# Expert 3's first weight chunks loaded early, and VectorE's selections moved ahead of the slot lists, in a two-layer trunk with a mixture of experts

## The chip, the cores and the metric

One core of a Trainium2 chip runs the whole program. The metric is the device time of one execution in microseconds (us); what is given is the median of several executions. The engines are TensorE (PE; its weight loads are PEld), VectorE (DVE), ScalarE (ACT), GpSimd (POOL) and SyncE (SP), which issues nearly all loads from device memory (HBM). Each engine runs its own instructions in order and waits on semaphores for the others.

## What is computed

512 tokens of width 1024 go through two layers and a last RMSNorm, all in float32. Layer 0 mixes tokens with a gated recurrence and chunked attention, layer 1 with a gated linear recurrence. Each layer then has a mixture of experts, which is where most of the time goes:

```python
h = h + mix
h = h + hier_moe(rms_norm(h, norm_ffn_g[layer]), router_group, router_expert, w_gate, w_up, w_down)

# hier_moe: 4 groups of 8 experts; top-1 group, then top-2 experts inside it, for every token
g_gate, g_idx = top_k(softmax(xt @ router_group), 1)
e_val, e_idx = top_k(logits of the 8 experts of that group, 2)
gate = g_gate * softmax(e_val)
for each of 32 experts e:                  # on the tokens that chose it
    hb = silu(xb @ w_gate[e]) * (xb @ w_up[e])   # w_gate, w_up: 1024 x 512
    y += gate * (hb @ w_down[e])                 # w_down: 512 x 1024
```

## The kernel before

**Experts.** The 32 experts are served one after another in both layers. Each has a list of at most 56 token slots (CAP). They go in groups of two (PICK): while group g is computed, the tokens of group g+1 are gathered. Gathering is a matmul of the tokens with a 0/1 matrix (times the norm's factor). VectorE writes that matrix (`selections(l, g)`, 8 instructions at L1657, into `me["sel"]`), TensorE multiplies (`pick`, L663, 64 matmul records a half, as 40 + 24 around the transpose), and VectorE copies the result out of PSUM with the norm's gain (`take_pick`, L1825). There is one `me["sel"]`, so selections of group g+2 can be written only when both halves of group g+1 have been picked.

For expert e, TensorE runs `gate_up` (L828: gate and up projections, 32 records), the first part of a `pick`, `turn` (L834: the transpose of the hidden rows), the rest of the `pick` and `out_rows` (L843: the down projection). Between them ScalarE takes silu (`silu`, L1306), VectorE multiplies (`hidden`, L1874) and copies the transpose (L1901), and at the end ScalarE (L1321) and VectorE (L1883) each copy half of the expert's rows to `me["rows"]`, from which GpSimd scatters them to device memory (`scatter_rows`, L1491). `me["rows"]` has two halves, used in turn, so the rows of expert 2 wait until the scatter of expert 0 has landed (`scattered[0]`).

**Lists.** GpSimd needs the table of row numbers. `slot_lists` (VectorE, L1839 to L1844) builds two operands from all tokens' places, `slot_table` (TensorE, L852 and L854, right after `gate_up` of expert 2) multiplies them, and `row_table` (VectorE, L1853 to L1861) turns the product into numbers (`table_ready`, on which GpSimd's first scatter waits) and also hands ScalarE the router's logits (`route_in`), for an Exp (L1367) behind its part of expert 2's rows.

VectorE's order is that of `dve_expert`: at expert 1 it does `take_pick`, `slot_lists`, `row_table`, its half of expert 1's rows (`out_rows`), and then `selections(l, 2)`, on which TensorE's first `pick` at expert 2 waits.

**Weights.** The three matrices of an expert, 2048 KB each, sit in slots of a ring of nine (`EXPERT_SLOTS`, three experts). SyncE issues the loads in one fixed order (`moe_loads`, L459 whole matrices, L493 pieces), each behind a wait for the matmuls that last read the slot: expert e's gate and up behind `gate_up` of expert e-3, its down behind `out_rows` of e-3. For experts 3 to 5 the loads are cut in pieces (`piece`), some released halfway through `gate_up` (`gu_half`).

**Start.** The program begins with the norm of x: TensorE transposes (`turn_rows`, L612), and ScalarE (`take_turned`, L1203, four instructions a half tile) and VectorE (`turned_rows`, L1603, one instruction a half tile) copy the transposes to `xT`, ScalarE tile 1, VectorE tiles 0, 2 and 3. The first projection (`proj0`, L736) needs all of `xT` and the first 2048 KB of its weights (L408).

## Time and profile before

| | |
|---|---|
| median of 3 executions | 1600.71 us (1599.98 to 1601.44) |
| the profiled execution | 1600.28 us, of which its span 1598.6 us |
| PE busy | 1541.1 us, 96% of the span |
| DVE, ACT, POOL busy | 554.0, 345.8 and 210.7 us |
| loads of SyncE's queue | 462.51 MB, 70.3% of what 16 DMA engines could be busy |
| mean granted TensorE clock | 0.994 of full speed |

The page cuts the span in 40 slices of 40 us. TensorE shows 9 tenths in nearly all of them, so the profile has to be read by what little TensorE waits for, and by the slices in which the DMA engines are as full: slices 10 to 18 and 31 to 39, within the experts, at 422 to 428 GB/s. Times in the rows below count from the span's start. A matmul of float32 shows as two records.

### The profile page before, as it was taken

The page shows a single profiled execution, that of the slowest core. Times are in us where ns is not written, and L with a number is a line of the kernel's source. Part 1 is how long each engine was busy: PE and PEld are TensorE (multiplying, and loading weights), DVE is VectorE, ACT ScalarE, POOL GpSimd, SP SyncE. Part 2 cuts the span into 40 slices and gives each one's busy share as a digit, 9 for nine tenths or more (in the row PEclk, how much of TensorE's full clock was granted, in tenths as well). Part 3 has the DMA queues.
Part 4 walks back from the last instruction along what each step waited for, and adds up shares of the span by engine and source line. Part 5 has one row for each costly group of instructions (what it writes and reads, how often), then busy time and mean ns, then how long its engine had stood idle before and what let it go on. Part 6 is the DMA issues. An engine that isn't in the chain of part 4 may idle for free. (4 is left out here: it accounts for less than half of the span.)

```text
span 1598.6 us, 26973 instructions
## 1 busy us (share of the span) xinstructions
PE 1541.1 (96%) x11592; PEld 794.0 (50%) x11592; DVE 554.0 (35%) x1277; ACT 345.8 (22%) x577; POOL 210.7 (13%) x256
## 2 busy tenths in 40 slices
PE   7999999999999999998999999999999999999997
PEld 4444545544444444443566666646454444444442
DVE  4222635322232222225254444445322222222225
ACT  3131621010000000003444555432010000000003
POOL 5000000000000000000244444420000000000000
PEclk9999999999999999999999999999999999999999
DMA  8711056999999999997421112115989999999996
GB/s 294 257 70 53 27 235 268 399 373 427 426 427 426 427 426 427 426 422 309 176 88 54 54 63 96 56 53 224 372 359 426 428 425 426 426 427 427 427 422 271
DMA packets 59403, 472.22 MB, mean 295 GB/s; under 512 B 12929, under 2 KB 12937, under 8 KB 31376
## 3 DMA queue, kind: packets, MB, share of 16 engines
q1 hardware_dynamic: 54336, 462.51, 70.3%
q0 software_dynamic: 4800, 7.87, 1.3%
q8 instruction: 95, 1.56, 0.4%
q14 instruction: 28, 0.23, 0.0%
q10 hardware_dynamic: 144, 0.05, 0.0%
HBM read 452.03 MB, written 24.27 MB: 298 GB/s over the span
## 5 line engine op out<-in xcount | busy, mean ns | idle before, releaser
L828 PE MATMUL ps<-sb_ring,sb_work 128*56 128x512 f32 x2048 | 451.6, 593 | 16.5 <-issue 13.3
L828 PEld LDWEIGHTS ps<-sb_ring,sb_work 128*56 128x56 f32 x2048 | 146.4, 130 | 308.3 <-issue 308.0
L663 PE MATMUL ps<-sb_work,sb_h 128*64 128x112 f32 x4096 | 225.1, 264 | 7.5 <-DVE sb_work L1657 7.5
L843 PE MATMUL ps<-sb_ring,sb_work 128*56 128x512 f32 x1024 | 230.8, 593 | 1.2 <-DMA sb_ring<-in_w_down_dram 1.2
L663 PEld LDWEIGHTS ps<-sb_work,sb_h 128*64 128x64 f32 x4096 | 207.2, 139 | 42.2 <-issue 30.9
L1491 POOL DMA_INDIRECT expert_rows<-sb_work,sb_ri x60 | 54.7, 912 | 1124.9 <-DVE sb_work L1883 1113.6
L1874 DVE TENSOR_TENSOR sb_work<-sb_work,ps 56x512 f32<-56x512 f32 x64 | 70.2, 1097 | 314.7 <-ACT sb_work L1306 314.6
L1069 PE MATMUL ps<-sb_work,sb_ring 128*128 128x512 f32 x384 | 172.3, 603 | 2.0 <-ACT sb_work L1203 2.0
L1306 ACT ACTIVATE sb_work<-ps 56x512 f32<-56x512 f32 x64 | 37.6, 588 | 441.8 <-PE ps L828 441.8
L843 PEld LDWEIGHTS ps<-sb_ring,sb_work 128*56 128x56 f32 x1024 | 67.1, 130 | 114.2 <-issue 112.0
L1321 ACT ACTIVATE sb_work<-ps 56x512 f32<-56x512 f32 x60 | 35.4, 590 | 395.1 <-PE ps L843 395.1
L1069 PEld LDWEIGHTS ps<-sb_work,sb_ring 128*128 128x128 f32 x384 | 71.7, 191 | 86.9 <-issue 86.0
L736 PE MATMUL ps<-sb_work,sb_ring 128*128 128x512 f32 x256 | 110.3, 592 | 1.7 <-DMA sb_ring<-in_ab_w_in_dram 1.7
L1883 DVE COPY sb_work<-ps 56x512 f32<-56x512 f32 x60 | 41.6, 693 | 188.3 <-ACT sb_work L1321 188.2
L736 PEld LDWEIGHTS ps<-sb_work,sb_ring 128*128 128x128 f32 x256 | 48.6, 190 | 62.6 <-issue 62.6
L2144 DVE COPY_PREDICATED sb_ring<-sb_tables,ps 128x512 f32<-128x512 uint32 x48 | 35.6, 742 | 93.5 <-PE ps L1087 92.7
L663 PE MATMUL ps<-sb_ring,sb_work 128*64 128x128 f32 x1120 | 64.3, 273 | 0.0
L663 PEld LDWEIGHTS ps<-sb_ring,sb_work 128*64 128x64 f32 x1120 | 60.9, 137 | 1.9 <-issue 1.9
L1657 DVE TENSOR_SCALAR sb_work<-sb_iota,sb_slot_key,sb_rstd 128x56 f32<-128x56 f32 x256 | 61.1, 308 | 0.3
L1825 DVE TENSOR_TENSOR sb_work<-ps,sb_fg 128x448 f32<-128x448 f32 x64 | 40.0, 625 | 59.6 <-PE ps L663 59.4
L1540 POOL TENSOR_TENSOR sb_ring<-sb_ring 128x256 f32<-128x256 f32 x56 | 48.6, 867 | 89.0 <-ACT sb_ring L1376 50.5
L628 PE MATMUL ps<-sb_ring,sb_work 128*128 128x512 f32 x128 | 59.5, 599 | 0.0
(240 smaller groups left out, 1216.2 us busy)
## 6 DMA issues: line engine op xcount, KB each, us to landing
sb_ring<-in_w_down_dram SPq DMA_DIRECT2D x62, 2048.0 KB, 24.4
sb_ring<-in_w_gate_dram SPq DMA_DIRECT2D x54, 2048.0 KB, 21.8
sb_ring<-in_w_up_dram SPq DMA_DIRECT2D x54, 2048.0 KB, 26.4
sb_ring<-in_w_gate_dram SPq DMA_DIRECT2D x18, 1024.0 KB, 10.5
sb_ring<-in_w_up_dram SPq DMA_DIRECT2D x18, 1024.0 KB, 12.8
sb_ring<-in_c_w_in_dram SPq DMA_DIRECT2D x8, 2048.0 KB, 9.0
sb_ring<-in_ab_w_in_dram SPq DMA_DIRECT2D x5, 2048.0 KB, 12.0
expert_rows<-sb_work SPq DMA_DIRECT2D x2, 4096.0 KB, 19.9
```

The source lines that it names most:

```text
L628: mm = nc.tensor.matmul(bank(job)[:], y[:, c, t * P:(t + 1) * P], wblock(s, NC)[:, c, :], start=(c == 0), stop=(c == NC - 1))
L663: mm = nc.tensor.matmul(dst[64 * z:64 * z + 64], a[:, 64 * z:64 * z + 64], b, start=start, stop=stop)
L736: mm = nc.tensor.matmul(dst[:], a, b, start=(c == 0), stop=(c == NC - 1))
L828: mm = nc.tensor.matmul(dst[64 * z:64 * z + CAP, :], me["xgT"][:, j, c, q * CAP:(q + 1) * CAP], wblock(slots[z], NC)[:, c, :], start=(c == ...
L843: mm = nc.tensor.matmul(dst[64 * z:64 * z + CAP, :], src[:, c * CAP:(c + 1) * CAP], wblock(slots[2], FC)[:, c, z * 512:(z + 1) * 512], sta ...
L1069: mm = nc.tensor.matmul(dst[:], w[:, c, k, :], xT[:, c, :], start=(c == 0), stop=(c == NC - 1))
L1491: return g.indirect_dma_start(out=y_d[l], out_offset=bass.IndirectOffsetOnAxis(ap=idx, axis=0), in_=me["rows"][0:CAP, j, :], in_offset=Non ...
L1540: g.tensor_tensor(qk[:, :, 0:m], kk[:, :, 0:m], e[:, :, 0:m], ALU.mult)
L1657: return v.tensor_scalar(dst, iota[:, 0:CAP], slot_key[:, t, e:e + 1], rstd[:, 2 * l + 1, t:t + 1], ALU.is_equal, ALU.mult)
L1825: drains(v.tensor_tensor(me["xgT"][:, g % 2, CB * b:CB * b + CB, :], bank(job)[:, 0:CB * PICK * CAP].rearrange("p (c s) -> p c s", c=CB), ...
L1874: return v.tensor_tensor(me["hrow"][0:CAP, :].rearrange("p (c q) -> p c q", c=FC), chunked(me["silu"][64:64 + CAP, :], FC), chunked(ps[moe ...
L1883: drains(v.tensor_copy(half_row(me["rows"][0:CAP, e % 2, :], 1), chunked(bank(("dn", l, e))[64:64 + CAP, :])), ("dn", l, e))
```

## The change

Three things are changed.

1. Chunk 0 (of eight) of expert 3's gate and up matrices, 128 x 512 elements (256 KB) each, is loaded to two free places in `work` (`ahead`), right behind the last load of expert 2 and with no wait for a slot; `gate_up` of expert 3 reads its first chunk there, behind a wait on `ahead_in`. The first piece of expert 3 in the ring is then chunk 1 alone.
2. VectorE's order at experts 1 and 2: `selections(l, 2)` stands right behind the `take_pick` of expert 1, ahead of `slot_lists`; `row_table` moves from expert 1 to expert 2, behind `hidden(l, 2)`.
3. At the start, the second half of tile 3 of `xT` is copied by ScalarE instead of VectorE.

```diff
--- before.py
+++ after.py
@@ -198,6 +198,7 @@
         me.update(carve(high, [("sel", (NT, PICK * ROW))]))
         me.update(carve(low[:, 2 * NC * PICK * CAP:], [("A", (2, NT, CAP))]))
         me.update(carve(high[:, 2 * D:], [("spread", (NT, NE))]))
+        ahead = (low[:, 7 * T:8 * T], high[:, T:2 * T])
         fin_g = tables[:, 0:D]
         fin_c = ring[:, 0, D:2 * D]
         hg = ring[:, 3, :].rearrange("p (t d) -> p t d", t=NT)
@@ -244,7 +245,7 @@
         out_ready, out_stored = [sem(f"out_ready{t}") for t in range(NT)], sem("out_stored")
         h_made = sem("h_made")
         zero_made, zero_out, attn_zero = sem("zero_made"), sem("zero_out"), sem("attn_zero")
-        gu_half = sem("gu_half")
+        gu_half, ahead_in = sem("gu_half"), sem("ahead_in")
         half_in = {(e, part): sem(f"half_in{e}_{part}") for e, part in HALVES}
         late_ready, fin_ready, hg_ready = sem("late_ready"), sem("fin_ready"), [sem(f"hg_ready{t}") for t in range(NT)]
 
@@ -493,8 +494,10 @@
                         sp.dma_start(ring[:, s, lo * 512:hi * 512], by_partition(w[l, e:e + 1])[:, lo * 512:hi * 512]
                                      ).then_inc(ring_in[s], 16)
 
+                for dst, w in zip(ahead, (w_gate, w_up)):
+                    sp.dma_start(dst, by_partition(w[l, 3:4])[:, 0:512]).then_inc(ahead_in, 16)
                 sp.wait_ge(gu_half, 4 * l + 1)
-                piece(3, 0, 2)
+                piece(3, 1, 2)
                 sp.wait_ge(gu_half, 4 * l + 2)
                 piece(3, 2, 4)
                 wait_full(sp, ("gu", l, 0))
@@ -820,13 +823,14 @@
             out_proj(0, w0_in[5:7], m0["y"], ([NC, NC, NC, NC - 1], [0, 0, 0, 0]))
 
 
-            def gate_up(l, slots, j, q, cs=range(NC), k=7):
+            def gate_up(l, slots, j, q, cs=range(NC), k=7, first=None):
 
                 dst = ps[moe_bank(l, k)]
                 for c in cs:
                     for z in range(2):
-                        mm = nc.tensor.matmul(dst[64 * z:64 * z + CAP, :], me["xgT"][:, j, c, q * CAP:(q + 1) * CAP],
-                                              wblock(slots[z], NC)[:, c, :], start=(c == 0), stop=(c == NC - 1))
+                        w = first[z] if first and c == 0 else wblock(slots[z], NC)[:, c, :]
+                        mm = nc.tensor.matmul(dst[64 * z:64 * z + CAP, :], me["xgT"][:, j, c, q * CAP:(q + 1) * CAP], w,
+                                              start=(c == 0), stop=(c == NC - 1))
                 return mm
 
             def turn_hidden(l):
@@ -895,7 +899,9 @@
                     if q == 0:
                         for b in range(PB):
                             wait_drained(pe, ("pick", l, g, b))
-                    mm = gate_up(l, three, g % 2, q, range(0, 4))
+                    if e == 3:
+                        pe.wait_ge(ahead_in, 32 * (l + 1))
+                    mm = gate_up(l, three, g % 2, q, range(0, 4), first=ahead if e == 3 else None)
                     if e == 2:
                         mm.then_inc(gu_half, 1)
                     fills(gate_up(l, three, g % 2, q, range(4, 8)), ("gu", l, e))
@@ -1183,6 +1189,7 @@
                     square(0, t, xs[:, t, :], xh[:, t, :])
                 act.wait_ge(vec_in, 16)
                 take_turned(0, 1)
+                take_turned(0, NT - 1, (1,))
 
             def norm_mid():
 
@@ -1193,9 +1200,9 @@
                 take_turned(2, 0)
                 take_turned(2, 1)
 
-            def take_turned(n, t):
-
-                for half in range(2):
+            def take_turned(n, t, parts=(0, 1)):
+
+                for half in parts:
                     job = ("xt", n, t, half)
                     wait_full(act, job)
                     for c in range(4):
@@ -1593,10 +1600,10 @@
                     src, dst = h[:, t, :].rearrange("p (c q) -> p c q", c=NC), chunked(xh2[:, t, :])
                 v.tensor_scalar(dst, src, rstd[:, n, t:t + 1], None, ALU.mult).then_inc(xh_ready, 1)
 
-            def turned_rows(n, t):
+            def turned_rows(n, t, parts=(0, 1)):
 
                 gain = at["mix_g"]
-                for half in range(2):
+                for half in parts:
                     job = ("xt", n, t, half)
                     c0 = (n // 2) * NC + half * 4
                     wait_full(dve, job)
@@ -1699,8 +1706,8 @@
                 if t == 1:
                     dve.wait_ge(vec_in, 16)
                     turned_rows(0, 0)
-            for t in range(2, NT):
-                turned_rows(0, t)
+            turned_rows(0, 2)
+            turned_rows(0, NT - 1, (0,))
             v.memset(m0["xa"][:, :, 0:3], 0.0).then_inc(dve_made, 1)
             dve.wait_ge(rtab_in, 16)
             v.tensor_copy(m0["rtab"][0:HEADS_B, 0:255], m0["rtab"][0:HEADS_B, 255:256].broadcast_to([HEADS_B, 255])
@@ -1895,6 +1902,8 @@
                 g, q = e // PICK, e % PICK
                 if e != 1:
                     hidden(l, e)
+                if e == 2:
+                    row_table(l)
                 wait_full(dve, ("ht", l, e))
                 if e > 0:
                     wait_full(dve, ("dn", l, e - 1))
@@ -1903,14 +1912,14 @@
                     hidden(l, 1)
                 take_pick(l, g + 1, q)
                 if e == 1:
+                    selections(l, g + 2)
                     slot_lists(l)
-                    row_table(l)
                 if e == 3:
                     gate_values(l)
                 if e == 4:
                     late_gates(l)
                 out_rows(l, e)
-                if q == PICK - 1 and g + 2 < NE // PICK:
+                if e > 1 and q == PICK - 1 and g + 2 < NE // PICK:
                     selections(l, g + 2)
 
             def last_hidden(l, e):
```

VectorE at expert 1, before, from the `take_pick` on to the first instruction of `row_table`:

```order
L1825 TENSOR_TENSOR sb_work<-ps,sb_fg 128x448
L1839 TENSOR_TENSOR sb_work<-sb_slot_key,sb_work 128x128
L1840 TENSOR_REDUCE sb_place<-sb_work 128x4
L1841 TENSOR_TENSOR sb_work<-sb_work,sb_tokval 128x128
L1839 TENSOR_TENSOR sb_work<-sb_slot_key,sb_work 128x128
L1840 TENSOR_REDUCE sb_place<-sb_work 128x4
L1841 TENSOR_TENSOR sb_work<-sb_work,sb_tokval 128x128
L1844 TENSOR_TENSOR sb_work<-sb_iota,sb_place 128x224 x2
L1853 TENSOR_REDUCE sb_top<-ps 128x1
```

and after the change:

```order
L1832 TENSOR_TENSOR sb_work<-ps,sb_fg 128x448
L1664 TENSOR_SCALAR sb_work<-sb_iota,sb_slot_key,sb_rstd 128x56 x8
L1846 TENSOR_TENSOR sb_work<-sb_slot_key,sb_work 128x128
L1847 TENSOR_REDUCE sb_place<-sb_work 128x4
L1848 TENSOR_TENSOR sb_work<-sb_work,sb_tokval 128x128
L1846 TENSOR_TENSOR sb_work<-sb_slot_key,sb_work 128x128
L1847 TENSOR_REDUCE sb_place<-sb_work 128x4
L1848 TENSOR_TENSOR sb_work<-sb_work,sb_tokval 128x128
L1851 TENSOR_TENSOR sb_work<-sb_iota,sb_place 128x224 x2
L1890 COPY sb_work<-ps 56x8x64
```

The eight instructions of `selections(l, 2)` now come first, and the rows' copy (L1883, now L1890) directly behind `slot_lists`.

VectorE from the end of `row_table` into expert 2, before:

```order
L1861 TENSOR_TENSOR sb_ex<-sb_ex,sb_rstd 128x20
L1883 COPY sb_work<-ps 56x8x64
L1657 TENSOR_SCALAR sb_work<-sb_iota,sb_slot_key,sb_rstd 128x56 x8
L1874 TENSOR_TENSOR sb_work<-sb_work,ps 56x512
L1901 COPY sb_work<-ps 128x224
```

and after the change, from the copy of expert 1's rows on:

```order
L1890 COPY sb_work<-ps 56x8x64
L1881 TENSOR_TENSOR sb_work<-sb_work,ps 56x512
L1860 TENSOR_REDUCE sb_top<-ps 128x1
L1861 TENSOR_SCALAR sb_flag<-sb_top 128x1
L1862 COPY sb_work<-ps 56x32
L1864 TENSOR_SCALAR sb_work<-sb_work 56x32
L1865 SCALAR_TENSOR_TENSOR sb_work<-sb_work 56x32
L1867 CAST sb_ri<-sb_work 56x32
L1868 TENSOR_TENSOR sb_ex<-sb_ex,sb_rstd 128x20
L1910 COPY sb_work<-ps 128x224
```

The seven instructions of `row_table` now stand between `hidden` of expert 2 (L1881) and the copy of its transposed rows (L1910), on which TensorE's down projection waits.

SyncE's loads from expert 2's up matrix to the second piece of expert 3, layer 0, with what they wait for, before:

```order
L459 DMA sb_ring<-in_w_up_dram 128x4096 [waits filled5]
L493 DMA sb_ring<-in_w_gate_dram 128x1024 [waits gu_half]
L493 DMA sb_ring<-in_w_up_dram 128x1024
L493 DMA sb_ring<-in_w_gate_dram 128x1024 [waits gu_half]
L493 DMA sb_ring<-in_w_up_dram 128x1024
L493 DMA sb_ring<-in_w_gate_dram 128x2048 [waits filled5]
L493 DMA sb_ring<-in_w_up_dram 128x2048
```

and after the change:

```order
L460 DMA sb_ring<-in_w_up_dram 128x4096 [waits filled5]
L498 DMA sb_work<-in_w_gate_dram 128x512
L498 DMA sb_work<-in_w_up_dram 128x512
L494 DMA sb_ring<-in_w_gate_dram 128x512 [waits gu_half]
L494 DMA sb_ring<-in_w_up_dram 128x512
L494 DMA sb_ring<-in_w_gate_dram 128x1024 [waits gu_half]
L494 DMA sb_ring<-in_w_up_dram 128x1024
L494 DMA sb_ring<-in_w_gate_dram 128x2048 [waits filled5]
L494 DMA sb_ring<-in_w_up_dram 128x2048
```

Two loads of 128 x 512 to `work` go out with no wait, and the two behind the first `gu_half` are half as long.

## Rows read from the trace of the kernel before

**Rows 1.** The list of TensorE's waits, whole span: us, times, longest us.

```profile
PE ps L828 <- issue: 13.3, 12, 3.1
```

**Rows 2.** TensorE in time, layer 0, experts 2 and 3: start, us, records, idle before.

```profile
300.61 7.04 PE L828 MATMUL ps<-sb_ring,sb_work 128*56 128x512 f32 x32
...
307.92 1.01 PE L854 MATMUL ps<-sb_work 128*56 128x32 f32 x16
312.72 3.61 PE L663 MATMUL ps<-sb_work,sb_h 128*64 128x112 f32 x40 [3.79 <-DVE sb_work L1657]
...
321.27 7.04 PE L828 MATMUL ps<-sb_ring,sb_work 128*56 128x512 f32 x32
328.13 2.09 PE L663 MATMUL ps<-sb_work,sb_h 128*64 128x112 f32 x40
330.20 0.42 PE L834 MATMUL ps<-sb_ident,sb_work 56*128 56x56 f32 x4
```

**Rows 3.** VectorE in time, layer 0, experts 1 and 2.

```profile
297.94 0.28 DVE L1839 TENSOR_TENSOR sb_work<-sb_slot_key,sb_work 128x128 f32<-128x128 f32 x1
...
299.88 0.69 DVE L1844 TENSOR_TENSOR sb_work<-sb_iota,sb_place 128x224 f32<-128x224 f32 x2
308.97 0.19 DVE L1853 TENSOR_REDUCE sb_top<-ps 128x1 f32<-128x32 f32 x1 [8.40 <-PE ps L854]
...
310.19 0.69 DVE L1883 COPY sb_work<-ps 56x512 f32<-56x512 f32 x1
310.80 1.86 DVE L1657 TENSOR_SCALAR sb_work<-sb_iota,sb_slot_key,sb_rstd 128x56 f32<-128x56 f32 x8
```

**Rows 4.** TensorE in time, layer 1, the same place.

```profile
1158.58 3.77 PE L663 MATMUL ps<-sb_work,sb_h 128*64 128x112 f32 x40 [3.75 <-DVE sb_work L1657]
```

**Rows 5.** Stretches, layer 0: PE, PEld, DVE, ACT, POOL busy; clock, DMA share, GB/s.

```profile
314.00:316.00 2.00, 2.00 (x28) 2.00 (x26) 0.00 (x0) 0.00 (x0) 0.00 (x0) 0.56 1.02 403
...
318.00:322.00 4.00, 4.00 (x21) 1.24 (x18) 0.62 (x1) 0.52 (x1) 0.00 (x0) 1.00 0.16 60
...
328.00:330.00 2.00, 2.00 (x42) 1.86 (x38) 1.03 (x1) 0.59 (x1) 0.00 (x0) 1.00 0.82 197
330.00:332.00 2.00, 2.00 (x36) 1.67 (x33) 0.47 (x3) 0.00 (x0) 0.00 (x0) 1.00 0.79 319
332.00:344.00 12.00, 12.00 (x88) 5.02 (x84) 4.98 (x16) 1.18 (x2) 0.91 (x1) 1.00 1.00 428
```

**Rows 6.** SyncE's issues in time: expert 5's down, expert 6's gate, expert 7's gate.

```profile
321.48 0.33 SPq L459 DMA_DIRECT2D sb_ring<-in_w_down_dram  x1
328.35 0.33 SPq L459 DMA_DIRECT2D sb_ring<-in_w_gate_dram  x1
...
342.27 0.33 SPq L459 DMA_DIRECT2D sb_ring<-in_w_gate_dram  x1
```

**Rows 7.** TensorE in time, layer 0: its first wait for weights.

```profile
600.76 7.08 PE L828 MATMUL ps<-sb_ring,sb_work 128*56 128x512 f32 x32 [0.58 <-issue]
```

**Rows 8.** ScalarE in time, layer 0: expert 2's rows, and the last table load behind them.

```profile
321.49 0.59 ACT L1321 ACTIVATE sb_work<-ps 56x512 f32<-56x512 f32 x1 [13.20 <-PE ps L843]
...
323.62 1.28 ACT L1306 ACT_TABLE_LOAD   x1
```

**Rows 9.** Line L1491: layer 0's first scatter and its landing; last row, all sixty.

```profile
L1491 POOL DMA_INDIRECT expert_rows<-sb_work,sb_ri x1: 1105/1105/1105, 311.1 to 311.1; - x1
...
DMA to landing us min/median/max: 7.2/7.2/7.2
...
DMA to landing us min/median/max: 5.6/8.0/9.3
```

**Rows 10.** TensorE in time: the last pick ahead of expert 0, both layers.

```profile
268.80 0.41 PE L693 MATMUL ps<-sb_work,sb_tri 128*128 128x32 f32 x2 [2.02 <-DVE sb_work L1645]
...
269.36 3.29 PE L663 MATMUL ps<-sb_work,sb_h 128*64 128x112 f32 x64
...
1113.20 0.41 PE L693 MATMUL ps<-sb_work,sb_tri 128*128 128x32 f32 x2 [2.02 <-DVE sb_work L1645]
...
1113.76 4.95 PE L663 MATMUL ps<-sb_work,sb_h 128*64 128x112 f32 x64
```

**Rows 11.** The start, in time: VectorE's last copies, and the first projection.

```profile
12.40 1.89 DVE L1603 TENSOR_TENSOR sb_work<-ps,sb_vec 128x512 f32<-128x512 f32 x3
...
14.89 0.67 PE L736 MATMUL ps<-sb_work,sb_ring 128*128 128x512 f32 x1 [1.66 <-DMA sb_ring<-in_ab_w_in_dram]
```

## The prediction

> **What bounds the kernel now.** TensorE is busy for 96% of the span, so I read only what it waits for, and then ask for each wait whether its end would pass through to the end of the layer. First the list of TensorE's waits. Its largest entry is 13.3 us in 12 waits at `gate_up`, put down to "issue" [rows 1]; in time the first of them in layer 0 comes at 600.8 us, late in the layer [rows 7], and they stand where an expert's weights have not landed: one expert takes TensorE 13.9 us (the gates of experts 6 and 7, released by `gate_up` of 3 and 4, go out at 328.35 and 342.27) [rows 6], while its three matrices (6.29 MB) take 14.7 us at the 428 GB/s that the full queue moves [rows 5]. TensorE begins each layer ahead of the loads, loses 0.8 us of that lead per expert, and is held by them for its last experts.
>
> So the time in TensorE alone says nothing; a wait early in a layer is worth only what it also moves the queue of loads. The stretches tell that: at 318 to 322 us the queue is nearly empty (60 GB/s), it has a second hole at 328 to 332 (197 and 319 GB/s), and from 332 on it is full [rows 5]. In the holes it is SyncE that waits, for slots: expert 5's down goes out at 321.48, when `out_rows` of expert 2 is done, and expert 6's gate at 328.35, when `gate_up` of expert 3 is done [rows 6]. Whatever delays TensorE before 328 us delays the whole queue behind expert 6, and so the end of the layer.
>
> Exactly there lies the wait that the change is about. In layer 0 TensorE ends `slot_table` at 308.93 and stands 3.79 us until VectorE has written the selections of group 2 [rows 2]; layer 1 has the same wait with 3.75 us [rows 4]. VectorE had been free, but it had `slot_lists`, `row_table` (which waits 8.40 us for TensorE's `slot_table`) and a copy of rows in front of them [rows 3].
>
> **The change: VectorE's order.** In the new order `selections(l, 2)` begins where `slot_lists` began, at 297.94, and takes 1.86 us [rows 3]: ready at 299.8, when TensorE needs it at 308.9. The wait goes, 3.79 us in layer 0 and 3.75 in layer 1. With it goes a second cost: after the wait the first 40 records of the pick took 3.61 and 3.77 us where those of expert 3 take 2.09 [rows 2, 4], and the granted clock at 314 to 316 us is 0.56 [rows 5]: after the idle stretch it stood for most of this pick at half, 1.2 GHz. Without the idle I take the pick of expert 3 as the price. That gives 1.52 and 1.68 us more. A last 0.18 us is the overlap of a pick with the matmuls before it (it starts at 328.13, they end at 321.27 + 7.04 = 328.31), which the wait had prevented. Sum: 3.79 + 1.52 + 0.18 = 5.5 us in layer 0, 3.75 + 1.68 + 0.18 = 5.6 us in layer 1.
>
> What is late next? `slot_lists` (297.94 to 300.57, 2.63 us) moves behind the selections, to 302.4; `slot_table` needs it when `gate_up` of expert 2 ends, 300.61 + 7.04 = 307.65 [rows 2, 3]. 5 us to spare, cost nothing. `row_table` (308.97 to 310.19, 1.2 us) moves behind `hidden` of expert 2. In expert 3 the transpose starts 1.9 us after the end of `gate_up` (328.31 to 330.20) and finds `hidden` done [rows 2], so in expert 2 `hidden` is done by 309.5 and `row_table` by 310.7, while the transpose itself, behind 2.09 us of pick, cannot end before 311.2. VectorE's copy of it, for which TensorE's down projection waits, is not delayed. Cost nothing, with 0.5 us of cover; a TensorE wait of some tenths if the cover is gone.
>
> **Does the queue follow?** Expert 6's gate goes out 5.5 us earlier, at 322.85. Before, the queue by then had run dry; now expert 5's down, issued at 316.0, still stands behind the pieces of expert 5, which end near 318.6 (318 to 322 moves 60 x 4 us = 0.24 MB, 0.56 us of full rate). Down takes 2.10 MB / 428 = 4.9 us, to 323.5. From issue to full flow a load on an empty queue needs about 1.3 us: of expert 6's 1.03 MB moved by 332 (197 x 2 + 319 x 2) full rate would take 2.4 us, 329.6, against the issue at 328.35 [rows 5, 6]. So expert 6 flows from 322.85 + 1.3 = 324.15, behind the 323.5 at which the queue is clear: TensorE still sets it, and the queue moves by the full 5.5 us. Thereafter it is full as before (expert 7's gate would go out at 336.8, expert 6's matrices last to 324.15 + 14.7 = 338.9). The waits at the end of the layer keep their length and come 5.5 us earlier. Layer 1 has the same rows and the same sum, 5.6 us.
>
> **The two chunks ahead.** They move 0.52 MB (1.2 us at 428 GB/s) out of the stretch that ends at 318.6. That would be worth 1.2 us if the queue set the start of expert 6; by the lines above it does not, by 0.65 us without the chunks and by up to 1.9 us with them. They are cover and no gain: 0, between 0 and 0.6 us a layer should the flow start later than I read it. Nor does TensorE need expert 3 earlier. The two loads that are left of the first piece are shorter, and two more loads are issued, each about the 0.33 us of SyncE's other issues [rows 6], before a wait that SyncE has anyway.
>
> All of this hangs on a queue that can run dry: it moves 428 GB/s when full, and has its holes at 318 and 328 us [rows 5]. A rule of the Trainium skill says otherwise. The page "DMA: Bandwidth & Descriptors" (section "Where 436 GB/s comes from") holds that for loads from device memory the memory's share of one core, about 358 GB/s, is what binds. By that estimate an expert's weights would take 17.6 us, the queue would never be empty, and the sum would be 0 instead of 11.1 us (rival (d)); by this the trace disagrees.
>
> **The start.** ScalarE's four copies of the last half tile replace one of VectorE's three, which end at 12.40 + 1.89 = 14.29 us. The projection starts at 14.89, on its weights [rows 11]. Four ScalarE copies after the last transpose cannot end much later than 14.4. Nothing, between -0.2 and +0.2 us.
>
> **Sum.** 5.5 + 5.6 = 11.1 us. The profiled execution took 1600.28 us (span 1598.6), so 1589.2; it lies 0.4 us under the median of 1600.71, and from that the forecast is **1589.6 us**.
>
> **Rivals.**
>
> (a) *ScalarE is late at expert 3.* Its half of expert 2's rows waits for the scatter of expert 0 (`scattered[0]`), and that for `row_table`, which now ends 0.5 us later in time while all of TensorE is 5.5 us earlier. The first scatter was issued at 311.1 and landed 7.2 us later, 318.3 [rows 9]: in the new order 318.8, after `out_rows` of expert 2 (316.0). Behind it ScalarE has the rows, Exp and two table loads, 3.4 us (321.49 to 323.62 + 1.28) [rows 8], to 322.2; silu of expert 3 is due at 322.8. Free by 0.6 us, plus what slack the transpose has. But landings range from 5.6 to 9.3 us, median 8.0 [rows 9]: at 9.3 ScalarE is free at 324.3, and TensorE would wait 1.3 to 1.5 us in each layer. Time: 1592.4.
>
> (b) *Slower than before*, by the same chain and beyond a point: if the scatter's landing, now in a fuller queue, took so long that TensorE stood as long as before with the clock halved again. A loss of 5.5 us less 1.6 for the clock is 3.9 us of wait, a landing of 311.6 + 12 us or later. At 14.5 us it waits 6.4, loses 1.6 to the clock and gives 2.5 us a layer away: 1605.7. Sixty landings, none over 9.3, speak against it.
>
> (c) *The queue follows only in part.* If 256 KB loads run less well than 512 KB ones, or the lag after an issue is longer, expert 6 starts up to 1 to 2 us later than reckoned: gain 7 to 9 instead of 11.1, 1592 to 1593.7.
>
> (d) *The change doesn't do what it says at the end of the layer*: the queue is never short of work, the loads set the end wholly, and the wait comes back there. 1600.7, no change. The holes of [rows 5] speak against it.
>
> (e) *The clock at the other wait.* Ahead of `positions` of the last tile TensorE idles 2.02 us in both layers; behind it the pick of 64 records takes 3.29 us in layer 0 and 4.95 in layer 1, at half the clock there [rows 10]. Everything in layer 1 comes earlier now, and this may fall out either way: 1.7 us less, 1587.9, or in layer 0 1.7 us more, 1591.3. The skill's page "TensorE: Matmul & The Clock Gate" (section "What's actually happening") says that the gate watches activity on a rhythm of its own, not started by the kernel, so that the same idle can fall on either side; that bears on this chance and on nothing else.
>
> **How the numbers follow.** Forecast, with its tenths: 0.65. (a) 0.08. (b) 0.03. (c) 0.10. (d) 0.03. (e) 0.09. Something that I don't see, either side: 0.02. From the bounds, (e) below and (c) above, the range is 1587.5 to 1593.7; it leaves out (b), (d) and the unseen. A measurement of this kernel can tell about 0.2% (3.2 us) from no change; all but (b), (d) and half of the unseen are faster by more: 0.93, no change 0.03, slower 0.04.
>
> **What the profile after would show.** No wait of TensorE at the pick of expert 2 in either layer, and 40 records in 2.1 us; the list of waits without the 7.5 us at L663; expert 6's gate issued near 322.9 instead of 328.35; no hole at 318 to 322, a smaller one before expert 6; the waits at the layer's end as long as before. Wrong if TensorE waits for ScalarE or VectorE at the transpose of expert 3, if the late waits grow by what the early one lost, or if expert 6's first bytes come later than 1.5 us after the issue.

## The result

| | before | after |
|---|---|---|
| median of the executions, us | 1600.35 (1598.77 to 1601.44, 4) | 1590.97 (1590.47 to 1591.31, 4) |
| the profiled execution, us | 1600.28 | 1590.47 |
| its span, us | 1598.6 | 1588.7 |

The ratio is 0.9942, with a 95% interval of 0.9925 to 0.9959: faster by 9.4 us, where 11.1 were forecast (1589.6, range 1587.5 to 1593.7). The direction, the place and the mechanism were right; the sum was 1.2 us too large by the spans, 1.7 us by the medians.

TensorE in time, layer 0, experts 2 and 3, after the change (start, us, line, records):

```profile
308.15 0.96 PE L858 MATMUL ps<-sb_work 128*56 128x32 f32 x15
...
309.00 2.11 PE L666 MATMUL ps<-sb_work,sb_h 128*64 128x112 f32 x39
311.04 0.46 PE L838 MATMUL ps<-sb_ident,sb_work 56*128 56x56 f32 x4
...
316.06 1.03 PE L832 MATMUL ps<-sb_work 128*56 128x512 f32 x4
316.91 6.18 PE L832 MATMUL ps<-sb_ring,sb_work 128*56 128x512 f32 x28
322.92 2.09 PE L666 MATMUL ps<-sb_work,sb_h 128*64 128x112 f32 x40
```

These answer to [rows 2]: the pick behind `slot_table` no longer waits, and 39 of its records take 2.11 us instead of 3.61 for 40. The four records that read `sb_work` alone are expert 3's first chunk from `ahead`. Layer 1 reads the same (before: [rows 4]):

```profile
1149.43 2.11 PE L666 MATMUL ps<-sb_work,sb_h 128*64 128x112 f32 x39
```

VectorE, layer 0 (before: [rows 3]). The selections, the end of `slot_lists`, `hidden`, the first and last of `row_table`, and the copy of the transpose:

```profile
298.17 1.83 DVE L1664 TENSOR_SCALAR sb_work<-sb_iota,sb_slot_key,sb_rstd 128x56 f32<-128x56 f32 x8
...
301.85 0.69 DVE L1851 TENSOR_TENSOR sb_work<-sb_iota,sb_place 128x224 f32<-128x224 f32 x2
...
308.55 1.07 DVE L1881 TENSOR_TENSOR sb_work<-sb_work,ps 56x512 f32<-56x512 f32 x1 [4.59 <-ACT sb_work L1313]
309.65 0.19 DVE L1860 TENSOR_REDUCE sb_top<-ps 128x1 f32<-128x32 f32 x1
...
310.68 0.17 DVE L1868 TENSOR_TENSOR sb_ex<-sb_ex,sb_rstd 128x20 f32<-128x20 f32 x1
311.53 0.39 DVE L1910 COPY sb_work<-ps 128x224 f32<-128x224 f32 x1 [0.69 <-PE ps L838]
```

`row_table` is done 0.69 us before the transpose is there: the cover that I put at 0.5 us.

The stretches of layer 0 (before: [rows 5]). Columns: PE, PEld, DVE, ACT, POOL busy; clock, DMA share, GB/s:

```profile
318.00:320.00 2.00, 2.00 (x12) 0.63 (x10) 0.14 (x1) 0.75 (x2) 0.00 (x0) 1.00 1.12 436
320.00:322.00 2.00, 2.00 (x12) 0.60 (x10) 0.55 (x1) 1.97 (x3) 0.15 (x1) 1.00 1.02 434
322.00:324.00 2.00, 2.00 (x30) 1.36 (x28) 0.24 (x1) 1.25 (x2) 0.76 (x1) 1.00 0.93 389
324.00:325.00 1.00, 1.00 (x22) 0.82 (x19) 0.86 (x1) 0.00 (x0) 0.00 (x0) 1.00 0.94 299
325.00:326.00 1.00, 1.00 (x20) 0.94 (x20) 0.39 (x1) 0.00 (x0) 0.00 (x0) 1.00 0.90 328
326.00:327.00 1.00, 1.00 (x20) 0.71 (x18) 0.22 (x1) 0.00 (x0) 0.00 (x0) 1.00 1.01 393
327.00:328.00 1.00, 1.00 (x8) 0.40 (x6) 0.90 (x5) 0.00 (x0) 0.00 (x0) 1.00 0.95 377
328.00:330.00 2.00, 2.00 (x13) 0.55 (x9) 0.26 (x2) 0.00 (x0) 0.00 (x0) 1.00 1.00 410
330.00:332.00 2.00, 2.00 (x12) 0.68 (x10) 1.11 (x4) 0.59 (x1) 0.00 (x0) 1.00 1.01 426
```

and SyncE's issues of expert 5's down and expert 6's gate (before: [rows 6]):

```profile
316.27 0.33 SPq L460 DMA_DIRECT2D sb_ring<-in_w_down_dram  x1
323.13 0.33 SPq L460 DMA_DIRECT2D sb_ring<-in_w_gate_dram  x1
```

The empty stretch at 318 to 322 us (60 GB/s) is full. Behind expert 6's issue a shallow hole is left: 299, 328, 393 and 377 GB/s in four us. What it costs is taken up with the run that loads expert 6 in halves. (The GB/s of these rows count all queues, GpSimd's scatters too.)

The waits of TensorE over the whole span, by line (busy us, mean ns, idle before). First two lines of before, then the same two of after:

```profile
L828 PE MATMUL ps<-sb_ring,sb_work 128*56 128x512 f32 x2048 | 451.6, 593 | 16.5 <-issue 13.3 <-DMA sb_ring<-in_w_up_dram 3.1
L843 PE MATMUL ps<-sb_ring,sb_work 128*56 128x512 f32 x1024 | 230.8, 593 | 1.2 <-DMA sb_ring<-in_w_down_dram 1.2
```

```profile
L832 PE MATMUL ps<-sb_ring,sb_work 128*56 128x512 f32 x2040 | 449.8, 593 | 17.7 <-issue 15.0 <-DMA sb_ring<-in_w_up_dram 2.6
L847 PE MATMUL ps<-sb_ring,sb_work 128*56 128x512 f32 x1024 | 230.8, 593 | 1.0 <-DMA sb_ring<-in_w_down_dram 1.0
L666 PE MATMUL ps<-sb_work,sb_h 128*64 128x112 f32 x4096 | 221.9, 262 | 0.0
```

The waits for weights grew, from 16.5 + 1.2 to 17.7 + 1.0 us: 1.0 us of what the picks gained came back at the end of the layers. The 7.5 us of waiting at the pick (L663, now L666) are 0.

For the rest I use one table. In each layer it counts from the start of `gate_up` of expert 0 and gives the start of `gate_up` of expert 3 and of expert 4, and the end of the experts (the first matmul at L993, in the changed kernel L999). Everything in it is from one profiled execution of each kernel. "Queue" is the time at which SyncE's loads have moved one fixed number of bytes (83 MB in layer 0, 309 MB in layer 1, some 97 us into the experts), counted from the packets of the trace (another way of counting them shifts all of a column by 0.1 to 0.2 us). Differences of some tenths between single executions say little.

| kernel | layer 0: exp. 3, exp. 4, queue, end | layer 1: exp. 3, exp. 4, queue, end |
|---|---|---|
| before | 48.50, 62.42, 99.68, 459.36 | 48.64, 62.57, 96.90, 459.22 |
| after | 43.06, 57.00, 94.53, 453.86 | 43.06, 57.01, 92.31, 454.61 |
| after, once more | 43.06, 57.00, 94.67, 454.33 | 43.06, 57.33, 91.84, 454.40 |
| new order, no chunks | 43.05, 57.00, 94.69, 454.14 | 43.06, 57.00, 92.89, 455.19 |
| chunks, old order | 48.62, 62.55, 99.81, 458.98 | 48.59, 62.52, 97.03, 461.12 * |
| start undone | 43.06, 56.99, 94.69, 454.66 | 43.05, 57.00, 92.12, 456.56 * |
| table kept at expert 1 | 44.33, 58.25, 95.77, 455.54 | 44.32, 58.24, 93.16, 459.49 * |
| table late | 43.05, 63.07, 98.98, 458.29 | 43.06, 62.51, 95.78, 458.17 |
| before + 8 matmuls | 50.24, 64.16, 101.36, 460.46 | 50.24, 64.18, 98.85, 462.20 * |
| before + 4 matmuls | 47.03, 60.98, 98.26, 457.50 | 47.00, 60.94, 95.34, 457.44 |
| after, expert 6 in halves | 43.01, 56.95, 94.02, 454.92 ** | 43.06, 57.11, 91.33, 453.94 |
| after + fillers of 4 | 43.06, 57.00, 94.34, 453.78 | 43.06, 56.99, 92.42, 458.25 * |
| after + fillers of 2 | 43.06, 57.00, 94.74, 454.18 | 43.06, 57.02, 92.50, 457.93 * |
| halves + fillers of 2 | 43.06, 57.00, 93.81, 453.04 | 43.06, 57.01, 91.30, 454.81 * |

\* with the clock at half behind a late wait for weights: it costs 1.5 to 1.7 us, but 2.8 to 3.0 us in three of them (start undone, table kept, fillers of 4), where the clock stayed at half longer; ** behind two.

The span of 1598.6 less 1588.7 is 9.9 us: 5.50 in layer 0's experts, 4.61 in layer 1's, less 0.23 by which this execution reached expert 0 later.

### The profile page after: what moved, and what is told of

Its sections match the earlier page's. It is cut to its first block and busy times, and to the rows that moved or that the text cites. A ratio compares the mean times of both kernels' runs of the same rounds, so it can differ in the third digit from the quotient of the medians.

```text
span 1588.7 us, 26982 instructions
## 1 busy us (share of the span) xinstructions
PE 1537.8 (97%) x11592; PEld 791.5 (50%) x11592; DVE 554.0 (35%) x1276; ACT 347.1 (22%) x581; POOL 210.2 (13%) x256
## 5 line engine op out<-in xcount | busy, mean ns | idle before, releaser
L832 PE MATMUL ps<-sb_ring,sb_work 128*56 128x512 f32 x2040 | 449.8, 593 | 17.7 <-issue 15.0
L666 PE MATMUL ps<-sb_work,sb_h 128*64 128x112 f32 x4096 | 221.9, 262 | 0.0
L666 PEld LDWEIGHTS ps<-sb_work,sb_h 128*64 128x64 f32 x4096 | 204.2, 138 | 34.4 <-issue 30.8
L1881 DVE TENSOR_TENSOR sb_work<-sb_work,ps 56x512 f32<-56x512 f32 x64 | 70.2, 1097 | 319.3 <-ACT sb_work L1313 319.2
L1890 DVE COPY sb_work<-ps 56x512 f32<-56x512 f32 x60 | 41.6, 693 | 194.4 <-ACT sb_work L1328 194.4
L666 PE MATMUL ps<-sb_ring,sb_work 128*64 128x128 f32 x1120 | 64.3, 273 | 0.0
L666 PEld LDWEIGHTS ps<-sb_ring,sb_work 128*64 128x64 f32 x1120 | 60.9, 137 | 1.9 <-issue 1.9
```

Of the source, the lines that this page charges most:

```text
L666: mm = nc.tensor.matmul(dst[64 * z:64 * z + 64], a[:, 64 * z:64 * z + 64], b, start=start, stop=stop)
L832: mm = nc.tensor.matmul(dst[64 * z:64 * z + CAP, :], me["xgT"][:, j, c, q * CAP:(q + 1) * CAP], w, start=(c == 0), stop=(c == NC - 1))
L1881: return v.tensor_tensor(me["hrow"][0:CAP, :].rearrange("p (c q) -> p c q", c=FC), chunked(me["silu"][64:64 + CAP, :], FC), chunked(ps[moe ...
L1890: drains(v.tensor_copy(half_row(me["rows"][0:CAP, e % 2, :], 1), chunked(bank(("dn", l, e))[64:64 + CAP, :])), ("dn", l, e))
```

## The experiments

**The changed kernel again**, no edit.

> The changed kernel once more, beside the kernel before and the three kernels that undo parts of it. In the two profiles its span is 9.9 us shorter (1598.6 to 1588.7), where 11.1 was forecast. Theory: the same 9 to 10 us here, 0.994 of the time before. If the missing 1.2 us were chance, it would come out nearer to 11.

Measured 1589.36 us (1588.02 to 1595.41, 6 executions; before, beside it, 1601.33), ratio 0.9933 (0.9919 to 0.9948). The mechanism repeats. TensorE in time, layer 1 at expert 3:

```profile
1164.05 0.43 PE L838 MATMUL ps<-sb_ident,sb_work 56*128 56x56 f32 x4 [0.33 <-DVE sb_work L1881]
```

Here rival (a) shows for once, 0.33 us. ScalarE's rows of expert 2, in the changed kernel:

```profile
319.24 0.59 ACT L1328 ACTIVATE sb_work<-ps 56x512 f32<-56x512 f32 x1 [10.72 <-DMA expert_rows<-sb_work,sb_ri]
...
321.38 1.28 ACT L1313 ACT_TABLE_LOAD   x1
323.14 0.59 ACT L1313 ACTIVATE sb_work<-ps 56x512 f32<-56x512 f32 x1 [0.48 <-PE ps L832]
```

ScalarE does wait for the scatter, and is free 0.48 us before silu of expert 3 is due (0.6 forecast). In layer 1 of this second execution the slack was used up.

**The order alone**, without the two chunks.

```diff
-                for dst, w in zip(ahead, (w_gate, w_up)):
-                    sp.dma_start(dst, by_partition(w[l, 3:4])[:, 0:512]).then_inc(ahead_in, 16)
                 sp.wait_ge(gu_half, 4 * l + 1)
-                piece(3, 1, 2)
+                piece(3, 0, 2)
```

> The changed kernel without the two chunks ahead: expert 3's first piece is two chunks in the ring again; VectorE's order and the start as changed. My prediction held the chunks to be cover and worth nothing (0 to 0.6 us a layer): same time as e1. Rival, from the trace after the change: the queue is still moving expert 5's down at 323.9 us when expert 6's gate was issued at 323.1, so the queue now sets expert 6's start, and without the chunks it starts up to 1.2 us later in each layer: 1 to 2.4 us slower than e1, and TensorE's waits at the layer's end longer by that.

Measured 1590.8 us (1588.74 to 1593.75), 0.9938 (0.9926 to 0.9950). The order brings the gain. Without the chunks the queue is where it was in layer 0 (94.69 against 94.53 and 94.67) and 0.6 to 1.0 us later in layer 1 (92.89 against 92.31 and 91.84); the layer's end is 0.6 to 0.8 us later there. Against three further kernels below that have the chunks and the same order (92.12 to 92.50) it is 0.4 to 0.8 us, and it is one execution without the chunks. By the time of the whole program the two can't be told apart.

**The chunks alone**, with the old order and the old start.

```diff
                 take_pick(l, g + 1, q)
                 if e == 1:
-                    selections(l, g + 2)
                     slot_lists(l)
+                    row_table(l)
```

> The kernel before plus the two chunks ahead alone: VectorE's order and the start as before. Theory: no gain (0, within 0.3 us), since the wait of 3.8 us at expert 2 stays and expert 6's gate is still issued late, at 328.3 us, on an empty queue. Rival (the chunks are what shortens the layer, the order is not): a gain of 2.4 us or more.

Measured 1599.37 us (1595.10 to 1602.43, 12 executions), 0.9991 (0.9980 to 1.0002): no difference that shows. TensorE, layer 0:

```profile
312.52 3.72 PE L666 MATMUL ps<-sb_work,sb_h 128*64 128x112 f32 x40 [3.79 <-DVE sb_work L1663]
```

The wait and the halved pick are those of [rows 2]. The chunks are no part of the gain in layer 0.

**The start undone**, VectorE again taking the half tile.

```diff
                 take_turned(0, 1)
-                take_turned(0, NT - 1, (1,))
```

> The changed kernel with the last half tile of xT copied by VectorE again, as before. Prediction: nothing, within 0.2 us. From the trace after: the first projection waits for ScalarE there and all of TensorE stands 0.2 us later up to expert 2 (269.03 against 268.80), so this should be 0.2 us faster than e1, at the edge of what can be seen; in its trace the first projection starts at 14.9 on its weights or at 14.4.

Measured 1590.7 us (1588.48 to 1593.66), 0.9939 (0.9926 to 0.9952). The first projection, first in the changed kernel, then with VectorE's copy back:

```profile
15.13 2.38 PE L739 MATMUL ps<-sb_work,sb_ring 128*128 128x512 f32 x5 [1.56 <-ACT sb_work L1210]
```

```profile
14.74 2.81 PE L739 MATMUL ps<-sb_work,sb_ring 128*128 128x512 f32 x6 [1.60 <-DVE sb_work L1609]
```

ScalarE's copies can be what the projection waits for, which I had excluded. But over all profiled executions the projection starts between 14.24 and 15.20 us with ScalarE's copies (mean of nine 14.88) and between 14.70 and 15.06 with VectorE's (mean of five 14.83). This edit is worth nothing that can be told.

**The table kept at expert 1**: the selections go ahead, `row_table` stays where it was.

```diff
                     selections(l, g + 2)
                     slot_lists(l)
+                    row_table(l)
```

> The changed kernel with row_table back at expert 1, behind slot_lists; selections stay ahead of both. It tells the two moves of VectorE apart. Theory: the selections alone take the 3.8 us wait away, but VectorE then stands at row_table until slot_table is done (309.2 us), does it (1.2 us), copies expert 1's rows (0.7) and only then does hidden of expert 2 (1.1): done near 312.2, where TensorE wants to transpose at 311.0. A wait of about 1.1 us at the transpose of expert 2 in each layer, and a time about 2 us over that of the changed kernel. If the place of row_table didn't matter: the same time, no wait.

Measured 1592.59 us (1589.71 to 1596.52), 0.9948 (0.9931 to 0.9966). TensorE at the transpose of expert 2, layer 0:

```profile
313.90 0.42 PE L838 MATMUL ps<-sb_ident,sb_work 56*128 56x56 f32 x4 [1.23 <-DVE sb_work L1881]
```

`row_table` waits for TensorE's `slot_table`, and the rows' copy and `hidden` stand behind it. Expert 3 starts at 44.33 instead of 43.06 in the table, and the end of layer 0 follows (455.54, which is 1.2 and 1.7 us later than in the two executions of the changed kernel). So the move of `row_table` is worth 1.27 us a layer at expert 3. It is the smaller part of the gain; moving the selections alone brings 4.2 of 5.4 us. The time of the whole program doesn't show the 2 us that were expected: its interval overlaps with those of the changed kernel.

**The table late**: `row_table` behind `take_pick` of expert 2, which delays GpSimd's first scatter by 3.6 us (315.39 us against 311.8).

```diff
-                if e == 2:
-                    row_table(l)
                 wait_full(dve, ("ht", l, e))
...
                 take_pick(l, g + 1, q)
+                if e == 2:
+                    row_table(l)
```

> The changed kernel with row_table later still, behind the take_pick of expert 2: it ends near 315.6 instead of 310.7 us. This puts a price on my rival (a)/(b), the chain from row_table over GpSimd's first scatter and ScalarE's rows of expert 2 to silu of expert 3. Theory: in the changed kernel ScalarE is free 0.5 us before silu of expert 3 is due, so 4.9 us more make silu 4.4 us late; TensorE waits about 4.2 us at the transpose of expert 3 in each layer, its clock is halved behind it (1.5 us more), and most of both comes through to the end: 8 to 11 us over the changed kernel, near the time of the kernel before. If the scatter doesn't hold ScalarE: no wait, the same time.

Measured 1597.93 us (1596.02 to 1602.14), 0.9990 (0.9977 to 1.0003): nearly all of the gain is gone. ScalarE, then TensorE at expert 3, layer 0:

```profile
324.10 0.59 ACT L1328 ACTIVATE sb_work<-ps 56x512 f32<-56x512 f32 x1 [15.73 <-DMA expert_rows<-sb_work,sb_ri]
```

```profile
329.35 0.63 PE L838 MATMUL ps<-sb_ident,sb_work 56*128 56x56 f32 x4 [4.48 <-DVE sb_work L1881]
329.91 2.51 PE L666 MATMUL ps<-sb_work,sb_h 128*64 128x112 f32 x24
```

The landing is 4.86 us later than in the changed kernel; less the 0.48 us of slack that gives 4.4 us, and the wait is 4.48 (3.83 in layer 1). The clock halves behind it (24 records in 2.51 us instead of 1.37). This is the chain of rivals (a) and (b), shown with its price: each us of landing beyond the slack is a us of TensorE. In layer 0 expert 4 starts 6.07 us later, but the queue only 4.4 and the layer's end 4.0 to 4.4 us: expert 6's gate and up had been issued on time, and only its down, behind `out_rows` of expert 3, came late. The hole in the queue is now there:

```profile
334.00:336.00 2.00, 2.00 (x12) 0.60 (x10) 0.00 (x0) 0.00 (x0) 0.00 (x0) 1.00 0.50 205
336.00:338.00 2.00, 2.00 (x12) 0.60 (x10) 1.18 (x4) 0.59 (x1) 0.00 (x0) 1.00 0.73 156
```

**The wait filled in the kernel before**, first with eight matmuls, later with four. Their product is not used; they are work added. The first run's fill, the second had 4 in place of 8:

```diff
                     if e == 2:
                         slot_table(l)
+                        fill(moe_bank(l, 2), 8)
...
+            def fill(bank_, n):
+                for _ in range(n):
+                    nc.tensor.matmul(ps[bank_][:], ident[:], h[:, 0, 0:512], start=True, stop=True)
```

> The kernel before with 8 matmuls of 512 columns (their result isn't used) between slot_table and the pick of expert 2, about 3.5 us, within the wait for the selections. It parts the two terms of my sum: the wait stays where it ends (312.7 us), but TensorE is busy in it. Theory: the granted clock is not halved behind it, the first 40 records of the pick take 2.1 us instead of 3.6 and 3.8, expert 3 starts 1.5 us earlier in each layer and the kernel is 2.5 to 3.2 us faster than before. If the slow pick had another cause: no change.

> The kernel before, with four matmuls of 128 x 512 (their product is not used; they add work and change no output) on TensorE between slot_table and the pick of expert 2, in the 3.8 us in which it waits for VectorE. In the run with eight of them a matmul took 0.89 us, so four take 3.6 us and end just before the selections are ready. Theory: the half clock behind the wait is the price of idling alone, and is worth 1.52 + 1.68 us. So no wait above 0.3 us at that pick, its first 40 records in 2.1 us in both layers, expert 3 starting 47.1 us after expert 0 (48.5 in the kernel before, 43.06 after the change), and about 3 us faster than before, 1597.5. Rival: the clock at that place does not hang on this idle stretch, or what it costs comes back at the end of the layer: 1600.5, as before.

Eight: 1603.14 us (1601.34 to 1606.79), 1.0022 (1.0012 to 1.0031). Four: 1597.45 us (1594.62 to 1600.37, 11 executions; before, beside it, 1599.47), 0.9984 (0.9973 to 0.9995). TensorE, layer 0, with eight and with four:

```profile
308.74 7.13 PE L851 MATMUL ps<-sb_h,sb_ident 128*128 128x512 f32 x16
315.80 2.14 PE L663 MATMUL ps<-sb_work,sb_h 128*64 128x112 f32 x40
```

```profile
309.02 3.70 PE L851 MATMUL ps<-sb_h,sb_ident 128*128 128x512 f32 x8
312.88 2.14 PE L663 MATMUL ps<-sb_work,sb_h 128*64 128x112 f32 x40 [0.16 <-DVE sb_work L1663]
```

Eight missed their aim: I had sized them by `gate_up`, whose matmuls take 0.44 us each, and these take 0.89. They outlast the wait by 3.3 us, and expert 3 starts only 1.6 to 1.7 us later, since the pick behind them has its full clock. Four fit the wait. The wait is as long as before, the pick takes 2.14 us, expert 3 starts 1.47 and 1.64 us earlier (forecast of the prediction for the clock: 1.52 and 1.68), and the layers end 1.9 and 1.8 us earlier. So the second term of the sum is confirmed by itself, on the kernel before, and it passes through to the end. The time of the program agrees as far as its interval goes: 2.0 us of 3 expected.

**Fillers at the waits of 2.0 us in the changed kernel**: ahead of `positions` of the last tile in both layers, and ahead of layer 1's first projection. First with four matmuls each, later with two.

```diff
                 pick_first(l, 1)
+                fill(moe_bank(l, 2), 4)
                 positions(l, NT - 1)
...
-            xT_ready(2)
+            xT_ready(2, (0,))
+            fill(bk.jobs["xt", 2, 0, 0][0], 4)
+            xT_ready(2, range(1, NT))
```

> The changed kernel with 4 matmuls of 512 columns (result not used, about 1.8 us) ahead of two waits of 2.0 us that are still there: at positions of the last tile in each layer, and between the layers ahead of the first projection of layer 1. Theory: behind each of these waits the clock is halved in some executions (at 746 and 1108 us in the profile after; at 746 alone in e1) and costs 1.7 us each time; filled, it is never halved: 1.7 to 3.4 us faster than the changed kernel, and with less spread between executions. If they only delay TensorE: the same or slower.

> The changed kernel with the same three fillers of two matmuls alone. With four matmuls they took 3.7 us and outlasted the waits by 0.7 to 1.6 us each. Theory: with two (1.8 us) nothing is outlasted, the pick of 64 records behind positions takes 3.3 us in both layers, and the time is that of the changed kernel's undisturbed executions, 1590, with less spread between them. Rival: 1591 and the same spread, because the half clock then falls on another wait (the 3.1 us for weights at the end of layer 1).

Four: 1591.11 us (1590.03 to 1593.43), 0.9943 (0.9926 to 0.9959), too long again by the same factor. Two: 1588.53 us (1585.24 to 1589.67), 0.9917 (0.9903 to 0.9932). The last tile of layer 1, TensorE in time, in the changed kernel and with fillers of two:

```profile
1107.92 0.41 PE L696 MATMUL ps<-sb_work,sb_tri 128*128 128x32 f32 x2 [2.01 <-DVE sb_work L1652]
...
1108.69 4.68 PE L666 MATMUL ps<-sb_work,sb_h 128*64 128x112 f32 x64
```

```profile
1103.71 1.98 PE L705 MATMUL ps<-sb_h,sb_ident 128*128 128x512 f32 x4
...
1106.36 3.29 PE L667 MATMUL ps<-sb_work,sb_h 128*64 128x112 f32 x64
```

From the end of layer 0's experts to `gate_up` of expert 0 in layer 1 it is 386.57 us in the changed kernel and 383.06 with the fillers, 3.5 us less. The two halvings are 3.0 of it: with the chunks alone, where neither wait halved the clock, this stretch takes 383.55 us. Of these only a part reaches the end. Layer 1's end comes 3.3 us later behind expert 0 (457.93 against 454.61), 1.7 of it because the clock now halves behind the 3.3-us wait for the weights of expert 30, the last but one, most of the rest by longer waits for weights before it, one of 2.43 us at expert 23 above all, which I can't explain: the queue as a whole is no later there. Comparing medians against the kernel before of the same chip, 10.9 us are gained where the changed kernel gained 9.4 and 12.0; by those intervals the fillers alone are not told apart from nothing.

**Expert 6 in halves**: its gate and up are loaded as two pieces each, the first released halfway through `gate_up` of expert 3.

```diff
-                for e in range(6, NS):
+                sp.wait_ge(gu_half, 5 * l + 5)
+                piece(6, 0, 4)
+                wait_full(sp, ("gu", l, 3))
+                piece(6, 4, 8)
+                wait_full(sp, ("dn", l, 3))
+                weight_load(l, 6, 2)
+                for e in range(7, NS):
...
-                    if e == 2:
+                    if e in (2, 3):
                         mm.then_inc(gu_half, 1)
```

> The changed kernel, with expert 6's gate and up loaded in halves, the first half released halfway through gate_up of expert 3 instead of at its end. In the changed kernel the load queue moves 299, 328, 393 and 377 GB/s in the four us behind 324 us and 389 in the two ahead, which against 425 is 0.95 us of full flow lost in layer 0 up to 332 us, and 1.0 us in layer 1. Theory: this hole is why the end of the layer came 0.4 to 0.9 us less early than expert 3 did. So no stretch of a us under 380 GB/s between 318 and 332 us, the end of the layer 0.6 to 1.0 us nearer to expert 0 than in the changed kernel (453.86 and 454.61 us behind its gate_up there) as long as the clock is full in it, and 1 to 2 us faster, about 1589. Rival: the queue is held elsewhere (expert 4's down at 302 us, the landing of single loads), the layer keeps its 453.9 us and more, and the time is that of the changed kernel, 1591.

Measured 1588.78 us (1587.78 to 1591.92), 0.9922 (0.9908 to 0.9935). The stretches of its layer 0 (all of it 1.1 us later in this execution):

```profile
322.00:324.00 2.00, 2.00 (x12) 0.59 (x10) 0.09 (x1) 1.97 (x3) 0.61 (x1) 1.00 0.92 393
324.00:325.00 1.00, 1.00 (x22) 0.95 (x20) 0.12 (x1) 0.79 (x2) 0.30 (x1) 1.00 1.10 467
325.00:326.00 1.00, 1.00 (x24) 0.92 (x20) 0.98 (x1) 0.00 (x0) 0.00 (x0) 1.00 0.81 328
326.00:327.00 1.00, 1.00 (x18) 0.84 (x16) 0.39 (x1) 0.00 (x0) 0.00 (x0) 1.00 1.02 393
327.00:328.00 1.00, 1.00 (x20) 0.82 (x18) 0.10 (x1) 0.00 (x0) 0.00 (x0) 1.00 0.99 397
```

The hole is halved, not closed: one us at 328 GB/s is left. The queue is 0.5 us earlier in layer 0 and 1.0 in layer 1 (0.65 and 0.5 against the second execution of the changed kernel), and layer 1's end, with a full clock in all three, comes at 453.94 instead of 454.61 and 454.40. So the hole behind expert 6's issue did hold the queue by 0.5 to 1.0 us, and the end of layer 1 by 0.5 to 0.7; layer 0's end can't be read in this execution, with two halvings of the clock in it. The time of the whole program is not told apart from the changed kernel's: the intervals overlap.

**Halves and fillers of two together.**

> The changed kernel with expert 6's halves as in the run beside it, and with two matmuls of 128 x 512 (product not used) on TensorE in each of the three stretches in which it waits 2.0 us: ahead of positions of the last tile in both layers, and ahead of layer 1's first projection. Two take 1.8 us. Theory: those 2.0 us halve TensorE's clock for the 1.6 us behind in some executions and not in others; with them filled it is never halved there, the slower executions go, and the median falls by about 1 us below the run beside it, 1588. Rival: the fillers end after the wait by some tenths each, and the clock is halved elsewhere instead, so the time is the same or 0.5 us worse.

Measured 1586.52 us (1584.25 to 1587.05), 0.9907 (0.9894 to 0.9921). On the same chip its slowest execution lies below the fastest of the halves alone (1587.78), so the fillers do bring something when the queue follows, some 2 us. It is faster than both kernels. Against the changed one the comparison is across chips, by the ratios to the kernel before: 0.9907 here, 0.9942 and 0.9933 there, which is 4 to 6 us; the interval of the first of these two doesn't meet this one's, that of the second just does (0.9919 to 0.9921).

## Why the prediction came out right, and where its sum was off

**The wait and the clock behind it**: right, with their sizes. Expert 3 starts 5.44 and 5.58 us earlier, against 5.5 and 5.6. The order alone brings it, the chunks don't, and filling the wait shows the clock's share by itself, 1.47 and 1.64 us.

**The lists and `row_table`**: right. `slot_lists` ended at 302.5 (302.4 said), 5.3 us early; the cover of `row_table` was 0.69 us (0.5 said).

**"So the queue moves by the full 5.5 us"**: this is the step that failed, by size. Expert 6's gate was issued at 323.13, as reckoned (322.85, plus the 0.23 us of this execution). But I had the queue clear of expert 5 0.65 us behind that issue (323.5), so that a lag of 1.3 us would end on an empty queue and everything would be set by TensorE. In fact there was more of expert 5 left: at the issue 0.45 MB (layer 0) and 0.57 MB (layer 1), counted from the packets, 1.1 and 1.3 us at 428 GB/s, as long as the lag itself. The old loads' tail and the new loads' beginning meet at 299 to 393 GB/s. Before, 0.04 MB were left at that point, and the issue found a dry queue. The traces agree with that: where under 0.1 MB was left (eight layers of the kernels with the old order), the first 1 MB of expert 6 had been moved 4.2 to 4.3 us behind the issue; where 0.26 to 0.72 MB was left, 4.5 to 5.2 us, but for one layer (0.36 MB and 4.3 us); the two kernels with expert 6 in halves are left out here. The reckoning also left out a scatter of GpSimd's rows: its 0.12 MB move at 323 to 326 us, in the middle of this change-over, while before the change they fell into the hole at 328 us. How the loss divides between the backlog and the scatter no run shows. So the loads follow by 5.15 and 4.6 us (by 5.0 and 5.1 in the second execution of the changed kernel) instead of 5.5 and 5.6, and the layers' ends by 5.50 and 4.61 (5.03 and 4.82). The rest returns as waits for weights, 1.0 us in the list. In the profiled execution layer 0 kept its whole gain, 1.0 of the missing 1.2 us is layer 1's, and 0.23 the later arrival at expert 0. That was rival (c) in kind, at about half its price, and it goes with the queue's own backlog where I had named the loads' size and the lag. The loads in halves, which win back 0.5 and 1.0 us of the queue, show that the place is this one.

**The chunks**: 0 was said, 0 to 0.6 as the range. Layer 0: 0 to 0.2 us, but not for the reason given. The prediction took their 0.52 MB out of the stretch that ends at 318.6. By the packets the queue is 0.5 MB ahead with them 2 us before expert 0 (47.26 against 46.74 MB) and no longer ahead 10 us behind its start (48.94 against 49.10 MB): the slots for the next pieces come free at the same times with and without them (issues at 7.1 and 10.5 us), so the lead is used up in waiting for them. That this term came out right in layer 0 was luck. Layer 1: 0.4 to 1.0 us of the queue by one execution without them, at or over the end of the range; with the old order they bring nothing there either (97.03 against 96.90).

**The start**: nothing, and so it was in the mean (0.05 us). The reason was half wrong: in the profiled execution the projection waited for ScalarE and not for its weights.

**Rival (a)**: 0.48 us of slack where 0.6 was said, a wait of 0.33 us in one of four layers. The late table shows that the chain exists, and that each us of it beyond the slack is a us of wait. **Rival (b)**: the same run is its test; a landing 4.86 us later brought the program to 0.9990 of the kernel before, so the point from which the change loses lies just beyond, near the 12 us said. **Rival (d)**: fell. The queue moves 434 GB/s where it moved 60. The 358 GB/s of the Trainium skill ("DMA: Bandwidth & Descriptors", "Where 436 GB/s comes from") are not what binds this program, which runs on one core: the full slices of every page here move 420 to 428.

**Rival (e)**: it happens, but it is no matter of this change. Over the eleven profiled executions without fillers at these waits, the clock halved behind the 2.0 us ahead of the last `positions` in two of layer 0's and seven of layer 1's, and behind the 2.0 us ahead of the first projection in seven; each time it cost 1.2 to 1.7 us. That goes with the spread of several us between executions of the same kernel: of the changed kernel's second run, the execution of 1588.02 us had a mean clock of 0.997, that of 1595.41 us 0.993. The two profiled executions of the result have the clock halved behind the same two of these three waits (the first projection's and layer 1's `positions`), and from layer to layer they take 386.53 and 386.57 us, so rival (e) has no part in their difference of 9.9 us. That they agree in this is chance. The Trainium skill's page "TensorE: Matmul & The Clock Gate" ("What's actually happening") says that the gate's rhythm isn't started by the kernel; that the same idle of 2.02 us goes either way agrees.

## What to carry to other kernels

When an early stall on the busiest engine goes, the loads move only as far as their own backlog lets them: at the place where they are next released, count the bytes still in the queue, and look for other engines' transfers there. Here 1.1 to 1.3 us of backlog cost the queue 0.3 to 1.0 us. An order among small instructions on an idle engine is worth looking at wherever the busy engine waits for the last of them, since one such wait can also cost the clock behind it (here 1.5 and 1.6 us behind 3.8). And split the load that is released at the thin place (0.5 to 1.0 us of the queue here), rather than load ahead of a place where the queue waits for slots, which used the lead up.

## What was not expected of the hardware

A float32 matmul of 128 x 128 by 128 x 512 took 0.89 us (7.13 us for eight), against 0.44 in `gate_up` (7.04 us for sixteen). There two products of 56 columns stand side by side, in rows 0 to 55 and 64 to 119 of the same PSUM bank; the trace shows that such a pair takes the time of one.

An idle of 2.0 us was enough to halve the granted clock in 16 of 33 cases; fillers (1.9 to 3.7 us) prevented it in all nine. The half clock of the pick shows in the changed kernel's stretches of layer 1, the clock in the third column from the end:

```profile
1107.00:1109.00 2.00, 1.08 (x8) 1.02 (x10) 1.20 (x8) 0.00 (x0) 0.00 (x0) 0.80 0.99 418
1109.00:1111.00 2.00, 2.00 (x26) 2.00 (x24) 0.60 (x3) 0.00 (x0) 0.00 (x0) 0.50 0.97 418
```

Half of full speed is the level of 1.2 GHz. With both neighbouring waits filled, the clock halved instead behind the wait of 3.3 to 3.4 us for expert 30's weights, in all three kernels with fillers, while of the eleven others it did so in four. Whether the fillers bring that about or chance, three executions don't settle.
